# Value projection with 512 moving columns out of two weight slots, in a two-layer encoder trunk

## The chip, the cores and the metric

The kernel runs on one core of one Trainium2 chip. The metric is the device time of one launch in microseconds (us); three runs before the change gave 1040.82, 1041.38 and 1041.64 us, median 1041.38.

## What is computed

Two layers of a streaming-encoder trunk on x of 256 tokens by 1024 features, all in float32. Each layer is:

```python
x = layer_norm(ALPHA * x + 0.5 * swiglu(x, w_gate, w_up, w_down))      # first feed-forward, F = 2816
h = x @ w_in                         # 1024 x 3072: q, k, v of 8 stick-breaking heads, q, k, v of 8 chunked heads
oa = stick_breaking_attention(qa, ka, va)                              # causal, heads of 64
ob = chunked_rel_attention(qb, kb, vb, rel_bias)                       # softmax in a band, chunks of 64
mixed = concat(head_rmsnorm(oa), head_rmsnorm(ob))
x = layer_norm(ALPHA * x + mixed @ w_out)
x = layer_norm(ALPHA * x + 0.5 * swiglu(x, ...))                       # second feed-forward
```

The part that changes is the product of x with the value columns of w_in (512 for each kind of head).

## The kernel before, in words

**Weights.** All weights come as a stream of units of 128 x 2048 float32 (1 MB). A unit of `w_in` holds 256 output columns for the whole contraction: eight chunks (`KC`) of 128 rows by 256 columns. Per layer there are 33 units for each feed-forward, 12 of `w_in` and 4 of `w_out`. The 12 units of `w_in` are numbered 0 to 11 in the order of `W_IN` (L76): q and k of the first kind of head, q and k of the second, then v of the first (units 8 and 9) and v of the second (10 and 11). The four of `w_out` are called units 12 to 15 here. A unit goes through one of three slots, given by `SLOT`: units 8 and 11 use slot 2, unit 9 slot 0, unit 10 and unit 12 slot 1.

**Splitting.** For precision each float32 number is split into a high and a low part. ScalarE copies a unit from `raw` to `w_hi` (L380), VectorE subtracts to make `w_lo` (L640). `three` (L891 to L895) then does three matmuls, high x high, low x high and high x low. ScalarE may overwrite a slot of `w_hi` only when TensorE has used the unit three before it (semaphore `unit_used`, L379); for unit 12 it waits for unit 10 (L391), which had the same slot. VectorE's split counts up `lo_ready`; SyncE's loads wait for that count (L264), so a raw slot is loaded again once the unit in it has been split.

**Projections.** The q and k units use `columns` (L897): the weights stand still and 256 tokens move. The v units use `rows` (L908): x stands still, one block of 128 tokens (`tb`) at a time, and 256 weight columns move; the two blocks write the two halves of one PSUM bank, and ScalarE copies it to `v` (L492). `w_in` (L1111) picks between them and may do half a unit at a time.

**Order.** The order of each engine is written by hand, in order: `attention` at L1117 for TensorE, L562 for ScalarE, L829 for VectorE. TensorE interleaves half units of projection with the small products of both attentions: `sb_scores` (q times k into bank 2 or 3), `sb_sums` (running sums of the softplus), `ca_scores` and `ca_turn` (scores and transposes of the softmax bands 0 to 5), `values` (probabilities times v), `head_means`. ScalarE does the exponentials, the evacuations and the high splits in one queue: `weights(l, 2)`, then the split of unit 9 (L582), `weights(l, 4)`, the split of unit 11 (L589), the evacuation of unit 9 (L590); near the end the split of unit 12 (L601), `turned(l, 4)` (L602), the evacuation of unit 11 (L603), `turned(l, 5)` (L604), then the first mixed operand (L605). TensorE's last `ca_turn(5)` waits for `turned(4)`, its last `values` for the evacuation and `turned(5)`. After them comes the output projection (L1158 to L1181), which moves 512 columns.

`last_used` (L993) is a place where TensorE waits for its own last matmul before it counts up a semaphore.

Of the kernel before, what the change touches and what calls it, by code (L numbers as in the profile page):

```python
# [28 lines left out]
P = 128  # L29
# [8 lines left out]
KC = D // P  # L38
# [17 lines left out]
def unit_slots():  # L56
# [6 lines left out]
    for s in order:  # L63
# [11 lines left out]

W_IN = [(kind, part, half) for kind, part in (("q", 0), ("k", 0), ("q", 1), ("k", 1), ("v", 0), ("v", 1))  # L76
        for half in range(2)]

SB_BANKS = [(1, (0, 1, 2, 3)), (0, (0, 1)), (0, (2, 3)), (1, (4, 5, 6, 7)), (0, (4, 5)), (0, (6, 7))]
SB_LATER = {1: 0, 2: 0, 4: 3, 5: 3}  # L80
# [17 lines left out]
def trunk(nc, x_in, xT_in, stream, ln_gb, mix_g, rel_band, out):  # L98
    ctx = ExitStack()
    with ctx:  # L100
# [6 lines left out]
        def sem(name):  # L107
            return ctx.enter_context(nc.semaphore(name))
# [85 lines left out]
        var_done = sem("var_done")  # L194
        lnv_done = sem("lnv_done")
        unit_evac = sem("unit_evac")
        z_done = sem("z_done")
        az_done = sem("az_done")
        ez_done = sem("ez_done")
# [36 lines left out]
        def split(l, rel):  # L236

            return l * UNITS + (rel + 4)
# [130 lines left out]
        def _(act):  # L369
# [101 lines left out]
            def band_out(l, i):  # L471
# [2 lines left out]
                                     bank[4 + i][:, :].rearrange("p (h s) -> p h s", h=2),  # L474
                                     ACT.Copy).then_inc(band_turned, 1)

            def evacuate(l, a):

                kind, part, half = W_IN[a]
                two = bank[a % 2][:, :].rearrange("p (c t) -> p c t", c=2)  # L480
                act.wait_ge(unit_used, used(l, ATT0 + a))
                if kind == "q":
                    nc.scalar.activation(qT[:, 4 * part + 2 * half:4 * part + 2 * half + 2, :], two,
                                         ACT.Copy, scale=QSCALE).then_inc(unit_evac, 1)
                elif kind == "k":
                    h0 = 8 * part + 4 * half
                    nc.scalar.activation(kpad[0:64, h0:h0 + 4:2, :], two[0:64], ACT.Copy)
                    nc.scalar.activation(kpad[64:128, h0 + 1:h0 + 4:2, :], two[64:128],
                                         ACT.Copy).then_inc(unit_evac, 1)
                else:  # L490
                    c0 = 512 * part + 256 * half
                    nc.scalar.activation(v[:, :, c0:c0 + 256], two, ACT.Copy).then_inc(unit_evac, 1)  # L492

            def log_keep(l, b):

# [66 lines left out]
            def attention(l):  # L562
                act.wait_ge(kzero, 1)
                split_hi_at(l, ATT0 + 1)
                split_hi_at(l, ATT0 + 2)
                for a in range(3):
                    evacuate(l, a)
                    split_hi_at(l, ATT0 + a + 3)
                evacuate(l, 3)
                split_hi_at(l, ATT0 + 6)  # L570
                log_keep(l, 0)
                softplus_hi(l, 0)
                for b in range(4):
                    log_keep(l, b + 1)
                    evacuate(l, 4 + b)
                    if b == 0:
                        weights(l, b)
                        softplus_hi(l, b + 1)
                    else:
                        softplus_hi(l, b + 1)  # L580
                        weights(l, b)
                    split_hi_at(l, ATT0 + 7 + b)  # L582
                softmax_exp(l, 0)
                log_keep(l, 5)
                evacuate(l, 8)
                softplus_hi(l, 5)
                softmax_exp(l, 1)
                weights(l, 4)
                split_hi_at(l, ATT0 + 11)  # L589
                evacuate(l, 9)  # L590
                weights(l, 5)
                softmax_exp(l, 2)
                softmax_exp(l, 3)
                square(l, 0, 0)
                square(l, 0, 1)
                softmax_exp(l, 4)
                evacuate(l, 10)
                head_rstd(l, 0, 0)
                head_rstd(l, 0, 1)
                softmax_exp(l, 5)  # L600
                split_hi_at(l, ATT0 + 12)  # L601
                turned(l, 4)  # L602
                evacuate(l, 11)  # L603
                turned(l, 5)  # L604
                mixed_hi(l, 0, 0)  # L605
                split_hi_at(l, ATT0 + 13)
                square(l, 1, 0)
                mixed_hi(l, 0, 1)
                square(l, 1, 1)
                split_hi_at(l, ATT0 + 14)  # L610
                head_rstd(l, 1, 0)
                head_rstd(l, 1, 1)
                split_hi_at(l, ATT0 + 15)
                mixed_hi(l, 1, 0)
                mixed_hi(l, 1, 1)
                split_first_hi(l, FFN_BASE[1], FILLED[FFN_BASE[1]])
# [273 lines left out]
        def _(pe):  # L890
            def three(o, w, x, start, stop):  # L891

                nc.tensor.matmul(o, w[0], x[0], start=start, stop=False)  # L893
                nc.tensor.matmul(o, w[0], x[1], start=False, stop=False)  # L894
                return nc.tensor.matmul(o, w[1], x[0], start=False, stop=stop)  # L895

            def columns(l, rel, slot, out_bank, halves=(0, 1)):  # L897

                pe.wait_ge(lo_ready, split(l, rel))
                for c in halves:  # L900
                    for kc in range(KC):
                        w = slice(kc * 256 + c * P, kc * 256 + (c + 1) * P)
                        last = three(out_bank[:, c * T:(c + 1) * T], (w_hi[:, slot, w], w_lo[:, slot, w]),
                                     (xT_hi[:, kc, :], xT_lo[:, kc, :]), kc == 0, kc == KC - 1)
                if halves[-1] == 1:
                    last.then_inc(unit_used, 1)

            def rows(l, rel, slot, out_bank, halves=(0, 1)):  # L908

                pe.wait_ge(lo_ready, split(l, rel))  # L910
                for tb in halves:
                    for kc in range(KC):
                        w = slice(kc * 256, (kc + 1) * 256)
                        t = slice(tb * P, (tb + 1) * P)
                        last = three(out_bank[:, tb * 256:(tb + 1) * 256], (xT_hi[:, kc, t], xT_lo[:, kc, t]),
                                     (w_hi[:, slot, w], w_lo[:, slot, w]), kc == 0, kc == KC - 1)
                if halves[-1] == 1:
                    last.then_inc(unit_used, 1)

            def down(slot, hi, lo, c0, tbs, start=False, stop=False, halves=(0, 1)):  # L920

# [141 lines left out]
            def values(l, part, i):  # L1063

                w = (stick_t, soft_t)[part]
                if part == 0:
                    pe.wait_ge(wm_done, l * 6 + 3 * (i + 1))
                    pe.wait_ge(unit_evac, l * WIN_UNITS + (9 + i))
                else:
                    pe.wait_ge(pt_done, l * 6 + 3 * (i + 1))  # L1070
                    pe.wait_ge(unit_evac, l * WIN_UNITS + (11 + i))
                for h in range(4 * i, 4 * i + 4):
                    rows_of = slice((h % 2) * HD, (h % 2 + 1) * HD)
                    c = (h // 2 % 2) * T
                    d = slice(512 * part + h * HD, 512 * part + (h + 1) * HD)
                    plain(O[part][i][rows_of, c:c + T], v[:, 0, d], w[:, h, 0:T], start=True)
                    last = plain(O[part][i][rows_of, c + P:c + T], v[:, 1, d], w[:, h, T:T + P], stop=True)
                last.then_inc(o_done, 1)
# [32 lines left out]
            def w_in(l, a, halves=(0, 1)):  # L1111
                if a >= 2 and halves[0] == 0:
                    pe.wait_ge(unit_evac, l * WIN_UNITS + (a - 1))
                f = rows if W_IN[a][0] == "v" else columns
                f(l, ATT0 + a, SLOT[ATT0 + a], bank[a % 2], halves)

            def attention(l):  # L1117
                first_columns(l, ATT0, phase(l, 1))
# [6 lines left out]
                w_in(l, 4, (1,))  # L1125
                sb_scores(l, 1)
                for b in range(4):
                    w_in(l, 5 + b, (0,))
                    sb_sums(l, b)
                    if b == 3:  # L1130
                        ca_scores(l, 0)
                    w_in(l, 5 + b, (1,))
                    sb_scores(l, b + 2)
                ca_scores(l, 1)
                w_in(l, 9, (0,))
                sb_sums(l, 4)
                ca_turn(l, 0)
                ca_scores(l, 2)
                w_in(l, 9, (1,))
                sb_sums(l, 5)  # L1140
                ca_turn(l, 1)
                ca_scores(l, 3)
                w_in(l, 10, (0,))
                values(l, 0, 0)
                values(l, 0, 1)
                ca_turn(l, 2)
                ca_scores(l, 4)
                w_in(l, 10, (1,))
                head_means(l, 0)
                ca_turn(l, 3)  # L1150
                ca_scores(l, 5)
                w_in(l, 11, (0,))
                ca_turn(l, 4)
                w_in(l, 11, (1,))
                ca_turn(l, 5)
                values(l, 1, 0)
                values(l, 1, 1)
# [105 lines left out]
```

## Time and profile before

| | |
|---|---|
| median of 3 runs | 1041.38 us (1040.82 to 1041.64) |
| span of the profiled execution, first to last instruction | 1038.6 us |
| the profiled execution's own time | only its span is given; the median above is 2.8 us over it |
| TensorE busy | 1020.4 us, 98% of the span |
| VectorE busy | 585.2 us, 56% |
| ScalarE busy | 503.7 us, 49% |
| HBM read | 183.51 MB, 178 GB/s over the span |

The attention stage of the first layer, from the `w_in` product to the end of the output projection, lies between about 205 and 322 us, that of the second between about 720 and 838 us. How to read the rows: times are us from the start of the span, the mean of one instruction in ns. PE is TensorE's matmul, PEld its weight load, ACT is ScalarE, DVE VectorE, POOL GpSimd. Matmuls overlap, so the duration of one is not its price: two successive starts give that.

### The profile page before, as it was taken

How to read it: one execution, taken by the hardware profiler on the slowest of the kernel's cores; microseconds unless marked ns; L12 is line 12 of the kernel's file. 1: busy time of each engine (PE TensorE's matmuls, PEld its weight loads, DVE VectorE, ACT ScalarE, POOL GpSimd, SP SyncE). 2: the span in 40 equal slices, each digit the busy share in tenths (PEclk: the TensorE clock that was granted, in tenths of full speed). 3: DMA queues.
4: the chain of work that ended last, by engine and by line, in shares of the span. 5: the costliest groups of instructions: out<-in, count | busy, mean ns of one | idle time of the engine just before them, and what ended most of it. 6: DMA issues, size and time to landing. Idle time of an engine off the chain costs nothing.

```text
span 1038.6 us, 18030 instructions
## 1 busy us (share of the span) xinstructions
PE 1020.4 (98%) x7128; PEld 943.2 (91%) x7128; DVE 585.2 (56%) x562; ACT 503.7 (49%) x552; POOL 28.3 (3%) x56
## 2 busy tenths in 40 slices
PE   6999999999999999999989999999999999999999
PEld 6999999799987999999889999997999889999997
DVE  4544544755788554544655454457457975444447
ACT  5444343557685344343543434346576754434335
POOL 3000000001100000000000000000010000000000
PEclk9999999999999999999999999999999999999999
DMA  8755555363325555555455545553623265545451
GB/s 333 282 195 185 179 201 166 119 244 122 123 82 209 202 197 174 189 190 175 161 198 210 185 180 201 172 192 129 232 88 122 87 239 203 187 179 198 171 195 42
DMA packets 34338, 185.24 MB, mean 178 GB/s; under 512 B 3824, under 2 KB 3824, under 8 KB 19440
## 3 DMA queue, kind: packets, MB, share of 16 engines
q1 hardware_dynamic: 32400, 174.60, 47.6%
q0 software_dynamic: 1744, 9.45, 2.5%
q8 instruction: 32, 0.52, 0.2%
q10 hardware_dynamic: 144, 0.52, 0.1%
q14 instruction: 18, 0.15, 0.0%
HBM read 183.51 MB, written 1.05 MB: 178 GB/s over the span
## 4 chain that ended last, share of the span: by engine, by line
PE 98%; DMA 1%; issue 1%; ACT 1%; DVE 0%; SPq 0%; ACTq 0%; DVEq 0%
PE bank L893 29%; PE bank L894 29%; PE bank L895 29%; PE bank L991 8%; PE bank L955 1%; PE bank L938 1%; DMA raw<-stream 1%; PE bank L1107 1%; ACT scratch L407 0%; PE bank L949 0%; DVE xn L715 0%; DVE xT_lo L660 0%; ACT xT_hi L398 0%; ACT w_hi L624 0%; ACT lt L410 0%
## 5 line engine op out<-in xcount | busy, mean ns | idle before, releaser
L640 DVE TENSOR_TENSOR w_lo<-raw,w_hi 128x2048 fp32r<-128x2048 f32 x158 | 361.6, 2292 | 244.8 <-ACT w_hi L380 239.7
L893 PE MATMUL bank<-xT_hi,w_hi 128*128 128x256 f32 x1568 | 444.6, 284 | 0.0
L894 PE MATMUL bank<-xT_lo,w_hi 128*128 128x256 f32 x1568 | 443.7, 283 | 0.0
L895 PE MATMUL bank<-xT_hi,w_lo 128*128 128x256 f32 x1568 | 443.7, 283 | 0.0
L380 ACT ACTIVATE w_hi<-raw 128x2048 fp32r<-128x2048 f32 x158 | 301.2, 1910 | 253.2 <-PE bank L895 241.0
L894 PEld LDWEIGHTS bank<-xT_lo,w_hi 128*128 128x128 f32 x1568 | 300.8, 192 | 1.6
L893 PEld LDWEIGHTS bank<-xT_hi,w_hi 128*128 128x128 f32 x1568 | 300.8, 192 | 1.6
L895 PEld LDWEIGHTS bank<-xT_hi,w_lo 128*128 128x128 f32 x1568 | 300.8, 192 | 0.0
L893 PE MATMUL bank<-w_hi,h_hi 128*128 128x512 f32 x320 | 125.0, 391 | 0.0
L894 PE MATMUL bank<-w_lo,h_hi 128*128 128x512 f32 x320 | 125.0, 391 | 0.0
L895 PE MATMUL bank<-w_hi,h_lo 128*128 128x512 f32 x320 | 124.5, 389 | 0.0
L450 ACT ACTIVATE h_hi<-scratch 128x512 fp32r<-128x512 f32 x40 | 25.3, 632 | 145.2 <-PE bank L895 129.4
L730 DVE SCALAR_TENSOR_TENSOR scratch<-scratch,bank 128x512 f32<-128x512 f32 x44 | 30.3, 688 | 80.1 <-PE bank L895 80.1
L895 PEld LDWEIGHTS bank<-w_hi,h_lo 128*128 128x128 f32 x320 | 60.1, 188 | 12.8
L893 PEld LDWEIGHTS bank<-w_hi,h_hi 128*128 128x128 f32 x320 | 60.2, 188 | 11.4
L894 PEld LDWEIGHTS bank<-w_lo,h_hi 128*128 128x128 f32 x320 | 60.2, 188 | 11.0
L735 DVE TENSOR_TENSOR h_lo<-scratch,h_hi 128x512 fp32r<-128x512 f32 x40 | 27.7, 691 | 69.7 <-ACT h_hi L450 69.7
L893 PE MATMUL bank<-w_hi,xT_hi 128*128 128x256 f32 (+1 forms) x192 | 64.7, 337 | 0.0
L895 PE MATMUL bank<-w_hi,xT_lo 128*128 128x256 f32 (+1 forms) x192 | 61.1, 318 | 0.0
L894 PE MATMUL bank<-w_lo,xT_hi 128*128 128x256 f32 (+1 forms) x192 | 61.1, 318 | 0.0
L893 PEld LDWEIGHTS bank<-w_hi,xT_hi 128*128 128x128 f32 x192 | 36.4, 190 | 4.0 <-issue 0.8
L894 PEld LDWEIGHTS bank<-w_lo,xT_hi 128*128 128x128 f32 x192 | 36.5, 190 | 3.0 <-issue 0.5
(127 smaller groups left out, 744.8 us busy)
## 6 DMA issues: line engine op xcount, KB each, us to landing
raw<-stream SPq DMA_DIRECT2D x110, 1024.0 KB, 4.8
raw<-stream SPq DMA_DIRECT2D x110, 512.0 KB, 4.5
lnp<-ln_gb POOLq DMA_DIRECT2D x6, 1024.0 KB, 5.0
soft_t<-rel_band POOLq DMA_DIRECT2D x2, 1024.0 KB, 11.4
xn<-x POOLq DMA_DIRECT2D x1, 1024.0 KB, 7.4
out<-xn SPq DMA_DIRECT2D x4, 256.0 KB, 2.1
qT<-xT SPq DMA_DIRECT2D x1, 512.0 KB, 4.9
qT<-xT ACTq DMA_DIRECT2D x1, 512.0 KB, 5.1
```

What stands on the lines that cost most here:

```text
L380: nc.scalar.activation(w_hi[:, slot, :], raw[:, slot, :], ACT.Copy).then_inc(hi_ready, 1)
L450: nc.scalar.activation(hi[:, :, :], hf.rearrange("p (c t) -> p c t", c=2), ACT.Copy).then_inc(hhi_done, 1)
L640: nc.vector.tensor_tensor(w_lo[:, slot, :], raw[:, slot, :], w_hi[:, slot, :].bitcast(F32), ALU.subtract).then_inc(lo_ready, 1)
L730: nc.vector.scalar_tensor_tensor(out=hf, in0=sg, scalar=0.5, in1=bank[1][:, :], op0=ALU.mult, op1=ALU.mult).then_inc(hf_done, 1)
L735: nc.vector.tensor_tensor(lo[:, :, :], hf.rearrange("p (c t) -> p c t", c=2), hi[:, :, :].bitcast(F32), ALU.subtract).then_inc(hlo_done, 1)
L893: nc.tensor.matmul(o, w[0], x[0], start=start, stop=False)
L894: nc.tensor.matmul(o, w[0], x[1], start=False, stop=False)
L895: return nc.tensor.matmul(o, w[1], x[0], start=False, stop=stop)
L938: last = nc.tensor.transpose(bank[2 * tb + half][:, q * P:(q + 1) * P], xn[:, tb, c:c + P], ident)
L955: nc.tensor.matmul(bank[3][:, :], ident, flat(table)[:, 0:512], start=True, stop=True)
L991: return nc.tensor.matmul(o, w, x, start=start, stop=stop, skip_group_check=True)
L1107: last = nc.tensor.transpose(bank[7][:, q * P:(q + 1) * P], ca_view(soft_t, b)[:, q // n, c:c + P], ident)
```

## The change

The value units are taken in pairs, (9, 8) and (10, 11). One matmul moves 512 columns: 256 out of each of two slots. A pair fills two banks, one for each token block, and is done in four parts: token block 0 with the first half of the contraction, then the second half, then token block 1 likewise. A part has 12 matmuls, where a half unit had 24. The first part waits for both units of the pair to be split. Both units are counted as used together, once the pair's last matmul has completed. The evacuation of a block writes 512 columns of `v` for one token block; where the slots' order is not that of the columns (pair 0) it takes two instructions. In TensorE's order the parts stand where the half units stood, except that the first part of the second pair moves behind `values(l, 0, 0)`. The orders of ScalarE and VectorE are otherwise as they were.

```diff
+V_PAIRS = [(9, 8), (10, 11)]
...
+            def evacuate_v(l, part, tb):
+
+                act.wait_ge(v_rows, l * 4 + (2 * part + tb + 1))
+                first, second = V_PAIRS[part]
+                c0, c1 = (512 * part + 256 * W_IN[a][2] for a in (first, second))
+                two = bank[tb][:, :].rearrange("p (c t) -> p c t", c=2)
+                out_v = v[:, tb, 512 * part:512 * part + 512].rearrange("p (c t) -> p c t", c=2)
+                if c0 > c1:
+                    nc.scalar.activation(out_v[:, 1, :], two[:, 0, :], ACT.Copy)
+                    nc.scalar.activation(out_v[:, 0, :], two[:, 1, :], ACT.Copy).then_inc(unit_evac, 1)
+                else:
+                    nc.scalar.activation(out_v, two, ACT.Copy).then_inc(unit_evac, 1)
...
-                evacuate(l, 8)
+                evacuate_v(l, 0, 0)
...
-                evacuate(l, 9)
+                evacuate_v(l, 0, 1)
...
-                evacuate(l, 10)
+                evacuate_v(l, 1, 0)
...
-                evacuate(l, 11)
+                evacuate_v(l, 1, 1)
...
-            def rows(l, rel, slot, out_bank, halves=(0, 1)):
...
+            def v_part(l, part, tb, kh):
+
+                units = V_PAIRS[part]
+                slots = [SLOT[ATT0 + a] for a in units]
+                if tb == 0 and kh == 0:
+                    pe.wait_ge(lo_ready, split(l, ATT0 + max(units)))
+                    pe.wait_ge(unit_evac, l * WIN_UNITS + (7, 9)[part])
+                if tb == 1 and kh == 0:
+                    pe.wait_ge(unit_evac, l * WIN_UNITS + (8, 10)[part])
+                t = slice(tb * P, (tb + 1) * P)
+                for kc in range(4 * kh, 4 * kh + 4):
+                    c = slice(kc * 256, (kc + 1) * 256)
+                    step = slots[1] - slots[0]
+                    hi, lo = (w[:, slots[0]:slots[1] + 1:step, c] for w in (w_hi, w_lo))
+                    out_v = bank[tb][:, :].rearrange("p (c t) -> p c t", c=2)
+                    last = three(out_v, (xT_hi[:, kc, t], xT_lo[:, kc, t]), (hi, lo), kc == 0, kc == KC - 1)
+                if kh == 1:
+                    last.then_inc(v_rows, 1)
+
+            def v_used(l, part):
+
+                pe.wait_ge(v_rows, l * 4 + (2 * part + 2))
+                pe.sem_inc(unit_used, 2)
...
-                    pe.wait_ge(unit_evac, l * WIN_UNITS + (9 + i))
+                    pe.wait_ge(unit_evac, l * WIN_UNITS + 10)
                 else:
...
-                    pe.wait_ge(unit_evac, l * WIN_UNITS + (11 + i))
+                    pe.wait_ge(unit_evac, l * WIN_UNITS + 12)
...
                 for b in range(4):
-                    w_in(l, 5 + b, (0,))
+                    if b < 3:
+                        w_in(l, 5 + b, (0,))
+                    else:
+                        v_part(l, 0, 0, 0)
                     sb_sums(l, b)
-                    if b == 3:
+                    if b < 3:
+                        w_in(l, 5 + b, (1,))
+                    else:
                         ca_scores(l, 0)
-                    w_in(l, 5 + b, (1,))
+                        v_part(l, 0, 0, 1)
                     sb_scores(l, b + 2)
                 ca_scores(l, 1)
-                w_in(l, 9, (0,))
+                v_part(l, 0, 1, 0)
                 sb_sums(l, 4)
                 ca_turn(l, 0)
                 ca_scores(l, 2)
-                w_in(l, 9, (1,))
+                v_part(l, 0, 1, 1)
+                v_used(l, 0)
                 sb_sums(l, 5)
                 ca_turn(l, 1)
                 ca_scores(l, 3)
-                w_in(l, 10, (0,))
                 values(l, 0, 0)
+                v_part(l, 1, 0, 0)
                 values(l, 0, 1)
                 ca_turn(l, 2)
                 ca_scores(l, 4)
-                w_in(l, 10, (1,))
+                v_part(l, 1, 0, 1)
                 head_means(l, 0)
                 ca_turn(l, 3)
                 ca_scores(l, 5)
-                w_in(l, 11, (0,))
+                v_part(l, 1, 1, 0)
                 ca_turn(l, 4)
-                w_in(l, 11, (1,))
+                v_part(l, 1, 1, 1)
+                v_used(l, 1)
                 ca_turn(l, 5)
```

## Rows read from the trace of the kernel before

**Rows 1.** The page: its head, TensorE's busy time, the chain by engine.
```profile
span 1038.6 us, 18030 instructions
PE 1020.4 (98%) x7128; PEld 943.2 (91%) x7128; DVE 585.2 (56%) x562; ACT 503.7 (49%) x552; POOL 28.3 (3%) x56
...
PE 98%; DMA 1%; issue 1%; ACT 1%; DVE 0%; SPq 0%; ACTq 0%; DVEq 0%
```

**Rows 2.** Groups by line and form: value projection, output projection (busy us, mean ns).
```profile
L893 PE MATMUL bank<-w_hi,xT_hi 128*128 128x256 f32 x128 | 38.5, 301 | 0.0
...
L893 PE MATMUL bank<-w_hi,xT_hi 128*128 128x512 f32 x64 | 26.2, 410 | 0.0
```

**Rows 3.** TensorE's timeline (start, us, engine, line): 32 narrow starts on, 25 wide ones.
```profile
212.05 0.28 PE L894 MATMUL bank<-xT_lo,w_hi 128*128 128x256 f32 x1
...
215.89 0.28 PE L893 MATMUL bank<-xT_hi,w_hi 128*128 128x256 f32 x1
...
310.12 0.39 PE L895 MATMUL bank<-w_hi,xT_lo 128*128 128x512 f32 x1
...
315.79 0.39 PE L893 MATMUL bank<-w_hi,xT_hi 128*128 128x512 f32 x1
```

**Rows 4.** Timelines of TensorE, ScalarE and VectorE where unit 8 begins.
```profile
256.79 0.47 PE L893 MATMUL bank<-w_hi,xT_hi 128*128 128x256 f32 x1
257.10 0.28 PE L894 MATMUL bank<-w_lo,xT_hi 128*128 128x256 f32 x1
...
254.88 1.91 ACT L380 ACTIVATE w_hi<-raw 128x2048 fp32r<-128x2048 f32 x1
...
256.82 2.29 DVE L640 TENSOR_TENSOR w_lo<-raw,w_hi 128x2048 fp32r<-128x2048 f32 x1 [1.73 <-ACT w_hi L380]
```

**Rows 5.** Timelines of ScalarE and VectorE, chain of waits (start, us), after unit 9.
```profile
271.40 1.90 ACT L380 ACTIVATE w_hi<-raw 128x2048 fp32r<-128x2048 f32 x1
...
273.99 2.29 DVE L640 TENSOR_TENSOR w_lo<-raw,w_hi 128x2048 fp32r<-128x2048 f32 x1
...
273.74 0.70 PE bank L991 x4
274.44 0.44 PE bank L1107 x4
274.88 0.89 PE bank L991 x8
278.63 2.80 PE bank L991 x32
```

**Rows 6.** TensorE's timeline where it waits for its own last matmul.
```profile
197.59 0.39 PE L895 MATMUL bank<-w_hi,hl_lo 128*128 128x512 f32 x1
198.27 1.09 PE L938 MATMUL bank<-table,xn 128*128 128x128 f32 x8 [0.30 <-PE bank L895]
```

**Rows 7.** Timelines of ScalarE and TensorE around the end of unit 11.
```profile
291.46 1.90 ACT L380 ACTIVATE w_hi<-raw 128x2048 fp32r<-128x2048 f32 x1
293.26 0.58 ACT L552 ACTIVATE soft_t<-bank 128x512 f32<-128x512 f32 x1
...
295.95 0.63 ACT L560 ACTIVATE xT_hi<-qT 128x512 fp32r<-128x512 f32 x1
...
294.78 0.60 PE L1107 MATMUL bank<-table,soft_t 128*128 128x128 f32 x4
295.31 2.87 PE L991 MATMUL bank<-soft_t,v 128*64 128x256 f32 x32
298.11 0.50 PE L893 MATMUL bank<-w_hi,xT_hi 128*128 128x512 f32 x1
```

**Rows 8.** A TensorE gap and the clock: timeline, stretch (clock after POOL), chain.
```profile
524.86 1.84 PE L991 MATMUL bank<-xT_hi,w_hi 128*128 128x256 f32 x8 [3.44 <-issue]
...
525.00:528.00 3.00, 3.00 (x16) 3.00 (x17) 0.17 (x1) 3.00 (x2) 0.00 (x0) 0.53 0.95 318
...
524.86 7.50 PE bank L991 x48
```

More of the change, by code:

```diff
@@ L196, in trunk @@
         unit_evac = sem("unit_evac")
+        v_rows = sem("v_rows")
         z_done = sem("z_done")
@@ L489, in evacuate @@
                                          ACT.Copy).then_inc(unit_evac, 1)
-                else:
-                    c0 = 512 * part + 256 * half
-                    nc.scalar.activation(v[:, :, c0:c0 + 256], two, ACT.Copy).then_inc(unit_evac, 1)
             def log_keep(l, b):
@@ L906, in columns @@
                     last.then_inc(unit_used, 1)
-            def rows(l, rel, slot, out_bank, halves=(0, 1)):
[L910 to L918, printed above, removed]
+            def v_part(l, part, tb, kh):
[18 more added lines that the diff above has]
+                pe.sem_inc(unit_used, 2)
             def down(slot, hi, lo, c0, tbs, start=False, stop=False, halves=(0, 1)):
@@ L1113, in w_in @@
                     pe.wait_ge(unit_evac, l * WIN_UNITS + (a - 1))
-                f = rows if W_IN[a][0] == "v" else columns
-                f(l, ATT0 + a, SLOT[ATT0 + a], bank[a % 2], halves)
+                columns(l, ATT0 + a, SLOT[ATT0 + a], bank[a % 2], halves)
             def attention(l):
```

## The prediction

> **What bounds the kernel now.** I read the page first. TensorE is busy for 98% of the span and 98% of the last-ending chain is TensorE [rows 1]; no other engine carries more than 1% of it. So time on TensorE counts one for one, gained or lost, and the other engines count only where they make it wait. Then the groups by form: the value projection is the 128 matmuls of 256 columns times three products, 384 over two layers, and the wide form of the same operands (the output projection) is already there with 512 columns [rows 2]. The "busy" of such a row is latency (301 or 410 ns); the price is the distance between starts, from TensorE's timeline. 32 matmuls of 256 columns take 3.84 us, 120 ns each; 25 of 512 columns take 5.67 us, 227 ns each [rows 3]. Last I laid the timelines of ScalarE and VectorE beside TensorE's around the value units. In the attention stage TensorE hardly waits (the chain shows no other engine there beyond a few tenths of a us), but the slack of each weight unit is small.
>
> **What the change gains.** 384 matmuls become 192 of double width: 2 x 120 - 227 = 13 ns each, 2.5 us in all. By parts: a half unit was 24 x 120 = 2.88 us, a new part is 12 x 227 = 2.72 us, 0.16 us less, eight parts per layer: **-1.27 us per layer**. The two-block moving operand and output (256 columns in each of two slots) are not in the trace. Bounds: 227 ns, as the contiguous wide row, and 240 ns, as two narrow ones (gain nil). I take 227, since width is what it shares with that row. ScalarE evacuates as much as before; only part 0 needs two instructions of 256 columns, between 0.58 (one copy of 512 [rows 7]) and twice that, 1.16 us; I take 0.70, since the columns are the same. No DMA is added, and loads are issued after the splits as before, so they shift with them.
>
> **What the change moves: three waits per layer.** A pair needs both units split before its first matmul, and gives both slots back only at its end.
>
> *Wait 1, unit 9.* Before, TensorE begins unit 8 at 256.79 and unit 9 only after all of unit 8 (2 x 2.88 us) and several small products. Now the part at 256.79 reads both. Unit 9's high half is split from 254.88 on ScalarE, its low half from 256.82 to 259.11 on VectorE [rows 4]. Nothing that is removed lies ahead of them: that split stands behind the weights of band 2, which need sums made in the middle of unit 7. TensorE stops from 256.79 to 259.15: **+2.36 us**. Behind it wait its own sums and scores; the softplus work of that time is already fed, and after the stop what ScalarE and VectorE do comes about 2 us later with it; I find no second stop there by the three timelines.
>
> *Wait 2, unit 11.* It shares slot 2 with unit 8. Unit 8 used to be free long before ScalarE split unit 11, at 271.40, when its queue got there [rows 5]. Now the slot is free only when the whole pair is done. Call S the time when the next matmul would start. The last product signals at S+0.2 (0.39 us long, 0.23 to the next start [rows 3], a handover of 0.03 as between the splits [rows 4]); split high 1.90, split low 2.29, with two handovers: S+4.5. TensorE has, before it wants unit 11: sums 0.70, turn 0.44, scores 0.89 and half the values, 1.40, so 3.4 us [rows 5]. **+1.1 us**. Inside it hides a second wait: the evacuation of the pair's second block stands behind the same split on ScalarE and ends at S+2.7, while the values want it at S+2.5 with the self-wait below. Only the later end counts. The self-wait: TensorE now waits for its own last matmul to pass the signal on. Where the kernel does this already, a start that would follow after 0.23 us follows after 0.68 [rows 6], one of six such places. These 0.45 us are covered by the evacuation and the split here and by wait 3 below; with that cover gone they would cost 0.45 each.
>
> *Wait 3, unit 12.* ScalarE's next split waits for unit 10 to be used. Before, that had long been so: it ran at 291.46, over TensorE's last half unit [rows 7]. Now units 10 and 11 are given back together at the end E of the last part, plus 0.2. So ScalarE stands still to E+0.2, and behind the split are queued the turned band 4, the evacuation of the last block and the turned band 5. TensorE's last turn wants band 4: split 1.80 (start to start, 291.46 to 293.26), copy 0.58 [rows 7]: E+2.6. It takes 0.5, the evacuation ends by then, and the values start at E+3.15 and take 2.80: the output projection starts at E+5.95. Before, it started at 298.11 with E at 294.78, so E+3.33 [rows 7]. **+2.62 us**. Next late would be unit 12's low half and the first mixed operand: low half done at E+4.4, and behind it the operand's low half at E+5.1 (a subtraction of 512 columns, estimated at 0.7 from 2.29 for 2048), before E+5.95. From there ScalarE and VectorE stand to TensorE as they did (the mixed operand's high half began 2.16 us before that start [rows 7], and now begins at about E+3.8, as much before), so nothing more is lost.
>
> After a wait, the switch that costs 0.2 us between two kinds of matmul is hidden in it (256.79 to 257.10 where 0.12 is usual [rows 4]): I take -0.1 at each of two waits, -0.2.
>
> **Sum.** Per layer -1.27 + 2.36 + 1.1 + 2.62 - 0.2 = +4.6; the second layer repeats the same stage with the same slack: +9.2 us. The profiled span is 1038.6, and the median of the runs shown, 1041.38, is 2.8 above it, which I leave. 1038.6 + 9.2 = 1047.8 on the span, **1050.7 us** as time.
>
> **Rivals.** (a) *The clock falls in the new stops.* In the one place where TensorE stood idle for 3.44 us, the granted clock of the next 3 us was 0.53 (mostly the lower level, 1.2 GHz), and the 48 matmuls there took 7.50 us [rows 8] instead of 48 x 120 ns = 5.76: 1.74 us. The new stops are about 2.2 and 2.5 us long, shorter than that one, so I don't expect it; but the light work around the second speaks for it. Two falls give 1054.2, four 1057.7. Chance 0.10. (The Trainium skill, "TensorE: Matmul & The Clock Gate", section "Why this matters for your kernels", asks that TensorE not be left idle between bursts of matmuls, since its clock then drops to half. The row of the 3.44 us gap agrees; the page speaks against this change.)
> (b) *The two-block operand costs as two narrow ones*: gain nil, 2.5 us more, 1053.2. For: no such access in the trace; against: splits by head in the sums run at their width's pace. Chance 0.07.
> (c) *Wait 3 is smaller*, because ScalarE's queue is otherwise than I read; without it 1045.4. Chance 0.05.
> (d) *The other side: a wide matmul costs less here than 227 ns.* Place: the 192 pairs; it decides when they gain 9.2 + 2.1 = 11.3 us more, 59 ns each, so from under 168 ns on. If width were free and each cost a narrow one's 120 ns, it would be 107 ns x 192 = 20.5 us less, 1030.2. Against it stand the wide matmuls of the trace at 227 [rows 3]. Chance 0.01. (The skill's same page, section "Back-to-back issue gap", gives 131 ns for 512 columns in a sustained stream; that would be 1032.3. The trace has 227, and the trace decides.)
> (e) *The waits are covered*: if unit 9 were ready by 256.8 and units 11 and 12 came early, only the gain stays: 1041.4 - 2.5 = 1038.9. That needs ScalarE to split unit 9 2.4 us sooner, and nothing in the change moves it. Chance 0.02.
>
> **How the numbers follow.** Forecast 0.75: 1050.7, with about 1 us either way for the evacuation and the handovers. The range takes in (b), the first of (a) and most of what lies between (c) and the forecast: 1047.8 to 1054.3. 0.2%, or 2.1 us, is what a measurement of this kernel can tell from no change. Slower than that hold the forecast, (a), (b) and (c): 0.96 with the rest shared; faster 0.03 with (d) and (e); between them 0.01.
>
> **What the changed profile would show.** Right: 192 matmuls of 512 columns on the value tiles at 227 ns from start to start; a TensorE gap of over 2 us released by VectorE's low split ahead of the first part in each layer; one of some 0.5 us released by the evacuation and one like it by the split of unit 11; ScalarE idle before the split of unit 12, and a TensorE gap of some 2.4 us before its last turn, released by ScalarE's copy of band 4. TensorE's busy time falls while the span grows, and its share drops below 98%. The stage from the first part to the end of the output projection is some 4.6 us longer in each layer, and no other stage changes. Wrong: no gap ahead of the first part (then unit 9 was ready), starts 240 ns apart (b), the granted clock below 1.0 behind a gap (a), or a difference outside the attention stage.

## The result, and the profile after

The changed kernel takes **1055.78 us** (four runs, 1052.67 to 1057.59), the kernel before 1041.33: a ratio of 1.0141, interval 1.0128 to 1.0154. It is slower, as forecast, but by 14.5 us where 9.3 was the forecast, and lies above the stated range, which ended at 1054.3. (One run in a later experiment, everything at once, took 1675.92 us beside ten of 1039.27 to 1042.15; it is left out of that ratio.)

The page of the changed kernel. Its lines are shifted: L906 to L908 are the three matmuls of `three`, L1016 the small products, L1132 the turns, L383 and L653 the high and the low split, L565 the copy of a turned band, L491 the evacuation of `v`.

```profile
span 1054.2 us, 17646 instructions
PE 1024.7 (97%) x6936; PEld 935.6 (89%) x6936; DVE 585.3 (56%) x562; ACT 503.8 (48%) x556; POOL 28.4 (3%) x56
...
PE 95%; ACT 2%; DVE 1%; issue 1%; DMA 1%; SPq 0%; POOL 0%; ACTq 0%; PEldq 0%; DVEq 0%; POOLq 0%
```

Beside [rows 1]: 192 fewer matmuls, as said, and 15.6 us more span. 1.0 us of it lies ahead of the first value part, where the two kernels do the same work. TensorE's busy time was to fall and rose instead, from 1020.4 to 1024.7 us; 3.2 us of that are the two falls of the clock shown below. Its share of the chain went from 98% to 95%; ScalarE has 2% of it where it had 1%, VectorE 1% where it had 0. TensorE's timeline (start, us, engine, line, what it read; in brackets how long it stood idle and what released it) has the stops of the first layer:

```profile
257.12 1.02 PE L1016 MATMUL bank<-qT,kpad 128*128 128x256 f32 x4
260.22 0.49 PE L906 MATMUL bank<-w_hi,xT_hi 128*128 128x512 f32 x1 [2.08 <-DVE w_lo L653]
...
261.59 0.63 PE L907 MATMUL bank<-w_lo,xT_hi 128*128 128x512 f32 x1
262.02 0.63 PE L908 MATMUL bank<-w_hi,xT_lo 128*128 128x512 f32 x1
...
277.75 0.39 PE L908 MATMUL bank<-w_hi,xT_lo 128*128 128x512 f32 x1
278.42 0.50 PE L1016 MATMUL bank<-sx_hi,neg_r 128*128 128x512 f32 x1 [0.28 <-PE bank L908]
...
282.63 0.49 PE L906 MATMUL bank<-w_hi,xT_hi 128*128 128x512 f32 x1 [0.29 <-DVE w_lo L653]
...
299.95 0.39 PE L908 MATMUL bank<-w_hi,xT_lo 128*128 128x512 f32 x1
303.16 0.63 PE L1132 MATMUL bank<-table,soft_t 128*128 128x128 f32 x4 [2.82 <-ACT soft_t L565]
303.72 0.65 PE L1016 MATMUL bank<-soft_t,v 128*64 128x256 f32 x3
```

The first line's four products take 0.68 us, so the first part could have started at 257.80 and starts at 260.22, behind VectorE's low split: wait 1, 2.42 us. The first pair ends with the matmul at 277.75, so S, where the next could start, is 277.98 (0.23 later). The self-wait follows it, and the second pair starts at 282.63 behind the split of unit 11: wait 2. The last turn starts at 303.16 behind ScalarE's copy of band 4: wait 3. Behind wait 1 stands what I had not counted on: the part that follows wait 1 has starts 0.43 us apart, not 0.23. The same stretch by windows (busy us by engine, then the granted clock as the third number from the end):

```profile
258.00:262.00 4.00, 1.92 (x6) 1.43 (x6) 2.78 (x2) 3.50 (x6) 0.41 (x1) 0.85 0.00 0
262.00:265.00 3.00, 3.00 (x10) 2.36 (x9) 0.69 (x1) 0.06 (x1) 0.00 (x0) 0.63 0.00 0
265.00:268.00 3.00, 3.00 (x19) 2.64 (x18) 1.64 (x4) 2.46 (x3) 0.64 (x1) 1.00 0.02 5
300.00:304.00 4.00, 1.18 (x9) 0.64 (x9) 1.44 (x1) 3.05 (x4) 0.00 (x0) 1.00 0.00 0
```

The clock fell to its lower level (1.2 GHz) just after the stop, in this layer and in the second one too (0.69 from 784 to 788). The part took 4.44 us; the next one, at the full clock, took 2.82, so a fall costs 1.62 us here. Behind wait 3, which was longer, the clock stayed at 1.00.

ScalarE's timeline at wait 3, the counterpart of [rows 7]:

```profile
300.62 1.91 ACT L383 ACTIVATE w_hi<-raw 128x2048 fp32r<-128x2048 f32 x1 [3.45 <-PEq L943]
302.44 0.58 ACT L565 ACTIVATE soft_t<-bank 128x512 f32<-128x512 f32 x1
302.91 0.59 ACT L491 ACTIVATE v<-bank 128x512 f32<-128x512 f32 x1
```

ScalarE stands idle for 3.45 us until TensorE's sequencer (L943, the release of both units) lets unit 12's split go; the copy of band 4 and the evacuation are queued behind it.

### The profile page after: what moved, and what is told of

It reads as the page before. It is cut to its first block, busy times and chain, and to the rows that moved or that the text cites. A ratio compares the mean times of both kernels' runs of the same rounds, so it can differ in the third digit from the quotient of the medians.

```text
span 1054.2 us, 17646 instructions
## 1 busy us (share of the span) xinstructions
PE 1024.7 (97%) x6936; PEld 935.6 (89%) x6936; DVE 585.3 (56%) x562; ACT 503.8 (48%) x556; POOL 28.4 (3%) x56
## 3 DMA queue, kind: packets, MB, share of 16 engines
HBM read 183.51 MB, written 1.05 MB: 175 GB/s over the span
## 4 chain that ended last, share of the span: by engine, by line
PE 95%; ACT 2%; DVE 1%; issue 1%; DMA 1%; SPq 0%; POOL 0%; ACTq 0%; PEldq 0%; DVEq 0%; POOLq 0%
PE bank L906 28%; PE bank L907 28%; PE bank L908 28%; PE bank L1016 7%; PE bank L980 1%; PE bank L963 1%; ACT w_hi L383 1%; DVE w_lo L653 1%; DMA raw<-stream 1%; PE bank L1132 0%; ACT scratch L410 0%; PE bank L974 0%; DVE xn L728 0%; DVE xT_lo L673 0%; ACT xT_hi L401 0%
## 5 line engine op out<-in xcount | busy, mean ns | idle before, releaser
L653 DVE TENSOR_TENSOR w_lo<-raw,w_hi 128x2048 fp32r<-128x2048 f32 x158 | 361.5, 2292 | 254.2 <-ACT w_hi L383 249.2
L906 PE MATMUL bank<-xT_hi,w_hi 128*128 128x256 f32 x1568 | 444.6, 284 | 0.0
L908 PE MATMUL bank<-xT_hi,w_lo 128*128 128x256 f32 x1568 | 443.7, 283 | 0.0
L383 ACT ACTIVATE w_hi<-raw 128x2048 fp32r<-128x2048 f32 x158 | 301.2, 1909 | 265.1 <-PE bank L908 242.8
L906 PEld LDWEIGHTS bank<-xT_hi,w_hi 128*128 128x128 f32 x1568 | 300.8, 192 | 1.6
L908 PEld LDWEIGHTS bank<-xT_hi,w_lo 128*128 128x128 f32 x1568 | 300.8, 192 | 0.0
L906 PE MATMUL bank<-w_hi,h_hi 128*128 128x512 f32 x320 | 125.0, 391 | 0.0
L908 PE MATMUL bank<-w_hi,h_lo 128*128 128x512 f32 x320 | 124.5, 389 | 0.0
L908 PEld LDWEIGHTS bank<-w_hi,h_lo 128*128 128x128 f32 x320 | 60.1, 188 | 12.7
L906 PEld LDWEIGHTS bank<-w_hi,h_hi 128*128 128x128 f32 x320 | 60.2, 188 | 11.5
L906 PE MATMUL bank<-w_hi,xT_hi 128*128 128x512 f32 x128 | 54.7, 428 | 4.5 <-DVE w_lo L653 4.5
L908 PE MATMUL bank<-w_hi,xT_lo 128*128 128x512 f32 x128 | 51.3, 401 | 0.0
L907 PE MATMUL bank<-w_lo,xT_hi 128*128 128x512 f32 x128 | 51.2, 400 | 0.0
L906 PEld LDWEIGHTS bank<-w_hi,xT_hi 128*128 128x128 f32 x128 | 24.8, 194 | 11.9 <-issue 6.6
L1016 PE MATMUL bank<-xT_hi,w_hi 128*128 128x256 f32 x96 | 17.0, 329 | 13.5 <-ACT w_hi L637 9.5
```

What stands on the lines that cost most here:

```text
L383: nc.scalar.activation(w_hi[:, slot, :], raw[:, slot, :], ACT.Copy).then_inc(hi_ready, 1)
L653: nc.vector.tensor_tensor(w_lo[:, slot, :], raw[:, slot, :], w_hi[:, slot, :].bitcast(F32), ALU.subtract).then_inc(lo_ready, 1)
L1016: return nc.tensor.matmul(o, w, x, start=start, stop=stop, skip_group_check=True)
```

## The experiments

All against the kernel before (1040.1 to 1040.9 us in these sets). "Stage" is the way from where the first value part could start to the output projection's first matmul: 41.32 us before (256.79 to 298.11), 48.73 in the changed kernel (257.80 to 306.53); in the second layer 41.34 and 48.49.

### Wait 1 alone, in the kernel before

```diff
                 for b in range(4):
+                    if b == 3:
+                        pe.wait_ge(lo_ready, split(l, ATT0 + 9))
                     w_in(l, 5 + b, (0,))
```

> The kernel before, with one wait added: TensorE waits for unit 9's low split where it begins unit 8. Nothing is widened and no slot is held longer. My theory now: wait 1 is a stop of 2.4 us per layer, and the clock falls behind it and costs 1.6 us more, so 2 x 4.0 = 8 us: about 1049.4 us, with the granted clock below 1.0 for some 3 us behind each stop. Rival (the fall came from something else in the changed kernel, such as the wide matmuls or the later stops): 2 x 2.4 = 4.8 us, about 1046.1, and the clock at 1.0 there.

Measured: 1046.12 us (1045.61 to 1046.78), 5.2 more. The stops are there with nothing widened. TensorE's timeline, then the windows behind the stop of each layer:

```profile
259.70 0.52 PE L893 MATMUL bank<-w_hi,xT_hi 128*128 128x256 f32 x1 [2.19 <-DVE w_lo L640]
```
```profile
260.00:264.00 4.00, 4.00 (x23) 4.00 (x23) 0.89 (x2) 1.19 (x2) 0.41 (x1) 0.60 0.02 4
...
779.00:783.00 4.00, 4.00 (x33) 3.91 (x34) 1.24 (x2) 2.08 (x5) 0.41 (x1) 1.00 0.01 4
```

The clock fell behind one stop and not behind the other, whose gap was 1.96 us. So neither of the two sums came out. The stage grew by 3.90 us in the first layer, where the clock fell (257.17 to 302.39), and by 2.15 us in the second, where it did not (776.52 to 820.01). Wide matmuls are not needed for a fall.

### The stops filled

First five constant matmuls ahead of the first part:

```diff
                     else:
+                        for i in range(5):
+                            nc.tensor.matmul(bank[4][:, :], ident, flat(table)[:, 0:512],
+                                             start=True, stop=True)
                         v_part(l, 0, 0, 0)
```

> The changed kernel, with five matmuls of constants (512 columns, 0.43 us each, 2.15 us in all) into an unused bank ahead of the first part, where TensorE stands still for 2.4 us. The first part starts when it did. If idleness brings the clock down and that costs 1.6 us per layer: 3.2 us less, about 1052.5, with the clock at 1.0 behind it. Rival (the fall is not from the stop): no change, 1055.8, and the clock falls as before.

Measured: 1058.19 us. I had taken one such matmul at 0.43 us, but each is two passes in the trace. The ten passes took 3.9 us, and the way to the first part grew from 2.42 to 4.07 us (256.99 to 261.06). The time says nothing of the clock's price. The profile still tells something: no fall at the filled stop in either layer, one behind the unfilled wait 3 of the first layer. Then with the size mended, and both stops filled:

```diff
+                        for i in range(2):
+                            nc.tensor.matmul(bank[4][:, :], ident, flat(table)[:, 0:512], ...)
                         v_part(l, 0, 0, 0)
...
                 v_used(l, 1)
+                pe.wait_ge(sa_done, l * 6 + 6)
+                for i in range(3):
+                    nc.tensor.matmul(bank[6][:, :], ident, flat(table)[:, 0:512], ...)
```

> The changed kernel, with constant matmuls of 512 columns into unused banks inside the two long stops: two ahead of the first part, three ahead of the last turn. One takes 0.86 us by the last fill (two passes of 0.43), so 1.7 us in a stop of 2.4 and 2.6 us in one of 3.2 from start to start; neither stop grows. If the clock falls because TensorE stands still: no fall in the attention stage of either layer, two falls fewer than in the changed kernel, 3.3 us less: 1052.5. Rival (falls come whatever TensorE does in the stops): 1055.8.

Measured: 1053.22 us (1052.70 to 1053.68). TensorE's timeline and the windows behind both stops:

```profile
258.06 1.88 PE L1156 MATMUL bank<-table 128*128 128x512 f32 x4
260.32 0.49 PE L906 MATMUL bank<-w_hi,xT_hi 128*128 128x512 f32 x1 [0.38 <-DVE w_lo L653]
```
```profile
261.00:265.00 4.00, 4.00 (x24) 3.40 (x22) 0.88 (x2) 2.06 (x4) 0.80 (x2) 1.00 0.02 4
...
303.00:309.00 6.00, 6.00 (x43) 4.56 (x39) 5.05 (x8) 5.23 (x6) 0.00 (x0) 1.00 0.52 176
```

The first part starts when it did, after the same wait, and the clock stays at 1.00 in the attention stage of both layers. The kernel takes 2.6 us less than the changed one, with 3.3 expected, and the runs lie within 1.0 us of each other, where those of the changed kernel lie 4.9 apart. The profiled run lost something elsewhere: behind the gap between the layers (3.50 us; [rows 8] show it for the kernel before) the clock was low twice as long as there, at 0.56 and 0.58 from 530 to 538. In the attention stage none of the six filled stops of these two kernels has a fall, so there standing still is what brings the clock down.

### Unit 9 split earlier

```diff
                 for b in range(4):
+                    if b == 2:
+                        split_hi_at(l, ATT0 + 9)
                     log_keep(l, b + 1)
...
-                    if b == 0:
+                    if b in (0, 2):
                         weights(l, b)
...
-                    split_hi_at(l, ATT0 + 7 + b)
+                    if b != 2:
+                        split_hi_at(l, ATT0 + 7 + b)
```

and the same for `split_lo_at` ahead of `softplus` on VectorE.

> The changed kernel, with unit 9 split one band earlier on ScalarE and VectorE (ahead of the softplus of band 3, and the weights of band 2 ahead of its high half). If wait 1 is the queue order on these two engines: stop and fall go, 2 x (2.4 + 1.6) = 8 us less, about 1047.7. Rival (a band's work is then late in its place and TensorE stops there instead): 1051 or more, with a new wait for the softplus or the weights.

Measured: 1048.17 us (1047.98 to 1048.55), 7.6 less than the changed kernel. The gap ahead of the first part is gone (its last small products start at 255.82, the part at 256.49), and no other came. In the profiled run the clock now fell behind wait 3, in both layers (0.63 from 298 to 302); the mean clock of its other three runs, 0.998, is that of the kernel before. So wait 1 came from the order of the two queues, and which stop the clock falls behind is not fixed.

### Narrow matmuls in the same order

```diff
-                    last = three(out_v, (xT_hi[:, kc, t], xT_lo[:, kc, t]), (hi, lo), kc == 0, kc == KC - 1)
+                    for i, slot in enumerate(slots):
+                        o = bank[tb][:, i * 256:(i + 1) * 256]
+                        plain(o, xT_hi[:, kc, t], w_hi[:, slot, c], start=kc == 0 and i == 0)
+                        plain(o, xT_lo[:, kc, t], w_hi[:, slot, c])
+                        last = plain(o, xT_hi[:, kc, t], w_lo[:, slot, c], stop=kc == KC - 1)
```

> The changed kernel, with each matmul of 512 columns done as two of 256, one for each slot; order, waits and evacuations as they are. By the starts in the two traces a wide part takes 2.94 us and a half unit 3.05, so 0.12 us for each of 16 parts: 1.9 us more, about 1057.7. Rival (the two-block access gives the width's gain away): 1055.8, the same.

Measured: 1056.00 us, from 1053.43 to 1058.72, where 1057.7 was expected. The falls hide an effect of this size (two runs with a mean clock of 0.998 took 1053.4 and 1053.7, two with 0.994 and 0.992 took 1058.3 and 1058.7). The traces decide. From the first part to the end of the first pair it is 259.69 to 278.29, 18.60 us, and 18.20 with wide ones (260.22 to 278.42); from the second pair's start to the last turn 20.95 against 20.53. Each pair of figures has the same falls in it. So width gains 0.1 us for each part, 0.8 us per layer, and the rival (no gain) is out.

### The last matmul counts the units itself

```diff
-                if kh == 1:
+                if kh == 1 and tb == 0:
                     last.then_inc(v_rows, 1)
+                if kh == 1 and tb == 1:
+                    last.then_inc(unit_used, 2)
...
-                v_used(l, 0)
```

and ScalarE's evacuation of the second block waits for `unit_used`.

> The changed kernel, where the pair's last matmul itself counts both units as used; TensorE no longer waits for itself, and ScalarE's evacuation of the second block waits for the same count. If the relay through TensorE's sequencer lies on wait 2 and wait 3 (ScalarE starts 0.28 us after the last matmul ended where 0.04 is usual): 0.24 us less at each of four places, 1 us in all, 1054.8; the idle 0.28 us at the end of the first pair goes, but TensorE then waits as long for the split. Rival (the self-wait is the price, 0.45 us at four places): 1.8 us less, 1054.0.

Measured: 1054.86 us (1054.78 to 1055.29), 0.9 less. All four runs have a mean clock of 0.995, and the two of the changed kernel with that clock took 1055.71 and 1055.85, so the falls don't explain it; the profile explains only half. ScalarE's split starts 0.16 us after the last matmul's end (299.67 + 0.39 to 300.22), not 0.28, and the output projection 0.13 us sooner. At the end of the first pair the idle 0.28 us became

```profile
280.48 1.57 PE L1016 MATMUL bank<-stick_t,v 128*64 128x256 f32 x16 [0.52 <-ACT v L492]
```

so the self-wait was covered by the evacuation, as predicted. Its price is the relay through TensorE's sequencer, some 0.1 us at each of four places, where 0.24 was expected; the time hit the expected 1054.8 in part by luck.

### Only one pair

```diff
-                v_part(l, 1, 0, 0)
+                w_in(l, 10, (0,))
...
-                v_part(l, 1, 1, 1)
-                v_used(l, 1)
+                w_in(l, 11, (1,))
```

with `rows` and `evacuate` for units 10 and 11 as before.

> The changed kernel, with units 10 and 11 back as four narrow halves, each unit counted as used on its own; only units 8 and 9 are a pair. If wait 3 is the late release of unit 10: the way from the end of the value projection to the output projection falls from 6.35 us to 3.33 as before; four narrow halves cost 0.1 us each more, and unit 11's split is not awaited any more, 0.3 less: 2.9 us per layer, 5.8 in all, 1050.0. Rival (the wait comes from the evacuation and the turned bands behind it): under 1 us per layer, 1054.

Measured: 1048.57 us (1047.63 to 1049.47), 7.2 less. TensorE's timeline around the end of unit 11:

```profile
297.48 0.60 PE L1147 MATMUL bank<-table,soft_t 128*128 128x128 f32 x4
298.00 2.87 PE L1031 MATMUL bank<-soft_t,v 128*64 128x256 f32 x32
300.81 0.50 PE L909 MATMUL bank<-w_hi,xT_hi 128*128 128x512 f32 x1
```

3.33 us, exactly as in [rows 7], where the changed kernel has 6.35. Wait 3 is the late release of unit 10. It is 1.4 us more than expected. Three of the four runs have a mean clock of 0.997, so a fall fewer than the changed kernel's profiled run (0.995), which can explain it. The run with 0.995 took 1049.47, 6.3 less than the changed kernel.

### What stands behind unit 12's split

```diff
-                split_hi_at(l, ATT0 + 12)
                 turned(l, 4)
                 evacuate_v(l, 1, 1)
                 turned(l, 5)
+                split_hi_at(l, ATT0 + 12)
```

> The changed kernel, where ScalarE does the turned band 4, the evacuation of the last block and the turned band 5 ahead of unit 12's high split, which stood before them. Calling the end of the value projection E, the output projection starts at E+6.35 in the changed kernel. If the split of unit 12 itself is the price of wait 3 (high 1.9, low 2.3, then the mixed operand's low half behind it on VectorE): the last turn and the values no longer wait, but the output projection does, and starts at E+6.3, with the gap now ahead of it: 1055.7, no change. Rival (the price is what stands behind the split on ScalarE): E+4.9, 1.5 us less per layer, 1052.8.

Measured: 1055.96 us, no gain (1052.88 and 1053.37 at a mean clock of 0.998, 1058.55 and 1058.58 at 0.994). TensorE's timeline:

```profile
300.21 0.63 PE L1132 MATMUL bank<-table,soft_t 128*128 128x128 f32 x4 [0.30 <-PE bank L908]
300.76 2.87 PE L1016 MATMUL bank<-soft_t,v 128*64 128x256 f32 x32
306.32 0.49 PE L906 MATMUL bank<-w_hi,xT_hi 128*128 128x512 f32 x1 [2.69 <-DVE xT_lo L839]
```

The last turn and the values run at once, and the same stop stands ahead of the output projection. E, the end of the value projection, is 299.75, so that starts at E+6.57. The price of wait 3 is the splitting of a unit that cannot start before the pair ends, not the queue behind it.

### The evacuation ahead of unit 11's split

```diff
-                split_hi_at(l, ATT0 + 11)
                 evacuate_v(l, 0, 1)
+                split_hi_at(l, ATT0 + 11)
...
                 values(l, 0, 0)
-                v_part(l, 1, 0, 0)
                 values(l, 0, 1)
+                v_part(l, 1, 0, 0)
```

> The changed kernel, with the second block of pair 0 evacuated ahead of unit 11's high split on ScalarE, and the first part of pair 1 behind both groups of values on TensorE. From the end S of pair 0 to the point where both groups of values and the first part are done it took 9.12 us. If wait 2 is that queue order: values start at S+2.5 without a gap, the second group at S+4.05 behind its weights, the part at S+5.5, end at S+8.45: 0.65 us less per layer, 1.3 in all, 1054.5. Rival (unit 11's split is late whatever the order): 9.1 again, 1055.8.

Measured: 1057.46 us (1052.80 to 1060.20), and by the trace S+9.66 (275.63 to 285.29), worse than the 9.12 it had. Both readings missed. The timelines of TensorE, GpSimd and VectorE:

```profile
280.93 1.57 PE L1016 MATMUL bank<-stick_t,v 128*64 128x256 f32 x16 [1.05 <-POOL stick_t L338]
...
278.94 1.94 POOL L338 TENSOR_SCALAR_AFFINE_SELECT stick_t<-stick_t 128x256 f32<-128x256 f32 x1 [4.79 <-ACT stick_t L531]
...
278.32 2.29 DVE L653 TENSOR_TENSOR w_lo<-raw,w_hi 128x2048 fp32r<-128x2048 f32 x1 [2.32 <-ACT w_hi L383]
```

The values began at once, as expected; their second group waited 1.05 us for GpSimd's causal mask, which took 1.94 us where the one before took 0.41. More on that below.

### Everything at once

The edits of four sections above together (unit 9 early, direct count, one pair, evacuation first), and unit 10's first half ahead of the values:

```diff
+                w_in(l, 10, (0,))
                 values(l, 0, 0)
-                w_in(l, 10, (0,))
                 values(l, 0, 1)
```

> Units 8 and 9 as a pair, 10 and 11 narrow; unit 9 split one band earlier, the pair's last matmul counts the units itself, the second block is evacuated ahead of unit 11's split, unit 10's first half stands before the values as in the kernel before. All three waits should be gone and the clock with them: the kernel before less the width's gain in four parts per layer, 8 x 0.1 = 0.8 us: 1040.2, beside 1040.9 of before. Rival (a new wait takes the place of one removed): above 1041.5.

Measured: 1040.28 us beside 1040.49, ratio 0.9999, interval 0.9989 to 1.0008. No stop is left in the attention stage, and the stage takes 41.11 us (256.54 to 297.65) where it took 41.32: 0.2 us less per layer, half of what I expected, too little for the times to tell. The gap between the layers varies as well: in this profiled run (1042.15 us) it was 4.70 us where the kernel before had 3.44, and the clock was low behind it for twice as long. What sets its length is open.

With both pairs kept, and the edits of unit 9 early, direct count, evacuation first and turned bands first:

> Both pairs kept, with unit 9 split one band earlier, the pairs counted by their last matmul, the second block evacuated first and ScalarE's bands ahead of unit 12's split. Waits 1 and 2 gone, wait 3 left as a gap of some 2.4 us ahead of the output projection, in part with a fall of the clock behind it. Against the kernel before, per layer: wait 3 +2.7, eight wide parts -0.8, so +1.9; 3.8 in all and 0 to 3.3 for the clock: 1044.3 to 1047.6, say 1046. Rival (with the other waits gone wait 3 is covered too): about 1039.

Measured: 1050.74 us (1050.03 to 1051.56), 4.7 more than expected. Wait 3 is there (2.42 us idle ahead of the output projection, released by VectorE), and the mask's wait, 1.61 us per layer, which I had not reckoned with: 3.2 of the 4.7 us. The rest is not accounted for. No version here beats the kernel before by more than a measurement can tell.

## Why the prediction was wrong, point by point

**The step that failed** is rival (a), put aside with "shorter than that one, so I don't expect it", chance 0.10. I read one idle row, 3.44 us with a fall behind it, as if it were a limit below which nothing happens. It only showed that such a gap is enough. Stops of 2.08 and 1.86 us idle brought the clock down in the changed kernel, one of 2.19 did and one of 1.96 did not in the kernel with the wait alone, and wait 3 (2.82) did in some kernels and not in the changed one's profiled run. The count varies from run to run, and so does the time. The mean clock of a run gives the count: in the profiled runs it is 0.998 with one fall (the kernel before has one, behind the gap between the layers), 0.997 with two, 0.995 with three, 0.994 with four.

Two falls at 1.62 us are 3.2 of the 5.1 us that were missing. Without them the kernel would have taken about 1052.5: 1.9 us above the forecast, inside the range. These 1.9 us are mostly the width and wait 3, which were mis-sized (below). The run of 1052.67, with a mean clock of 0.997, had one fall fewer than the profiled run's 0.995, which is 1.6 of the 3.1 us between the two. The Trainium skill ("TensorE: Matmul & The Clock Gate", section "Why this matters for your kernels") warns of idle gaps between bursts of matmuls, but the gaps it names are longer than these, so the prediction read too much into it where it says that the page speaks against the change. The warning was right in kind, and the trace has falls behind shorter gaps (1.86 and 2.08 us). A chance of a tenth was too little.

**The terms**, per layer, first layer of the profiled run:

| term | predicted | trace |
|---|---|---|
| width, eight parts | -1.27 | -0.8 (narrow against wide in the same order) |
| wait 1 | +2.36 | +2.42 (second layer 2.21) |
| wait 2 | +1.1 | +1.3 (unit 11's part at S+4.66, not S+4.5) |
| wait 3 | +2.62 | +3.02 (E+6.35, not E+5.95) |
| switch hidden in a wait | -0.2 | -0.2 (second start after 0.33 us, not 0.42) |
| clock | 0 | +1.6 |
| sum | +4.6 | +7.3; the stage grew by 7.41 |

*Width* was over-sized by 0.5 us per layer: a narrow matmul starts 119.5 ns after the one before it (22 intervals in 2.63 us), not 120, and a wide one of the value parts 229 ns, on average over the parts at full clock, not 227. Bounded rightly between 227 and 240, taken at the optimistic end. *Wait 1* was right: unit, place, releaser and size, and the unit 9 kernel shows that the order of two queues is all of it. *Wait 2* was right in shape; the self-wait was covered, as the direct count showed. *Wait 3* was right in cause (one pair takes it away), under-sized by 0.4 us: the signal relayed through TensorE lets ScalarE start 0.28 us after the last matmul's end, where I took 0.03, and the turn starts 0.14 us after the end of the copy. I had named "next late" rightly, unit 12's low half and the mixed operand: with the bands moved ahead, the stop went just there. The second layer did repeat the first (stage +7.15 us).

Rivals (b), (c), (d) and (e) are out: starts are 229 ns apart and not 240, wait 3 was not smaller, no part's starts averaged under 227 ns, and no wait was covered. What stays open is what decides whether the clock falls behind a given stop: 18 of the 30 open stops of 1.86 to 2.82 us in the profiled runs had a fall behind them, and their length does not sort them.

## What to carry to other kernels

Taking two operands in one instruction needs both earlier and frees both later: price those two dates in the queues of the engines that prepare and reuse the slots before counting what the wider instruction saves (here 0.8 us against 6.7 us of stops per layer). On a kernel bound by TensorE, reckon with a fall of the clock, 1.6 us here, behind each new stop of the size seen here (1.86 to 2.82 us; 18 of 30 had one), and expect the times to scatter. When a queue is reordered, ask what its last item is for: moving an evacuation ahead of a split moved a mask into VectorE's way.

## What the runs showed that I had not expected

**GpSimd's causal mask waits for VectorE's split.** The same mask on the same 128 x 256 elements takes 0.41 us alone and up to 1.94 us while a low split of 2.29 us runs. In the five kernels looked at (before, changed, direct count, evacuation first, two pairs) it ends 0.27 us after that split, whatever its own start: 278.94 + 1.94 against 278.32 + 2.29 in the rows above; 1.31 us in the kernel before (275.24, its split ends at 276.28). VectorE's split was never longer than 2.29 us. The Trainium skill says why ("SBUF — State Buffer", section "SBUF: two separate sides"): a VectorE operation with two SBUF inputs holds, for its whole length, a port pair that a GpSimd operation reading SBUF needs too. These ends agree; no run moved the split alone. In the kernel before this was hidden under half a unit of TensorE work; it became a stop of 1.05 to 1.61 us as soon as the order took that cover away.

**The clock makes the times scatter.** The kernel before lay within 2.4 us in all sets; kernels with two open stops per layer lay as far as 7.4 us apart (1052.80 to 1060.20, mean clock 0.998 to 0.990, the longer the lower). Filled stops brought the scatter back to 1.0 us. An effect under 2 us in such a kernel is read from the trace or not at all.
